# A quarter of the V rows of two tiles moves from TensorE to ScalarE and GpSimd, in a hybrid decoder step

## The reference

```python
q = (hb @ wq).astype(jnp.float32).reshape(chunk, PEER_HEADS, 2, PEER_HALF)
s = jnp.einsum('nhcd,hckd->nhck', q, sk)
sv, si = lax.top_k(s, PEER_TOPK)
...
expert = i1 * N_KEYS + i2
g = jax.nn.softmax(cs, axis=-1)
act = jax.nn.gelu(jnp.einsum('nd,nhkd->nhk', hb, u_tab[expert]).astype(jnp.float32), approximate=False)
return jnp.einsum('nhk,nhkd->nd', (g * act).astype(hb.dtype), v_tab[expert])
```

## Time and profile before

| | us |
|---|---|
| three runs, median | 3117.82 |
| lowest and highest | 3115.86, 3122.54 |
| the profiled execution | 3122.88 |
| its span, first to last instruction | 3121.1 |

### The profile page before, as it was taken

How to read it: one execution, slowest core, us unless ns; L and a number is a source line. 1 busy time by engine, 2 the same in 40 slices (tenths; PEclk the granted TensorE clock), 3 DMA queues, 4 the chain that set the end, 5 groups by cost and what they waited for, 6 DMA issues and landing times.

```text
span 3121.1 us, 28094 instructions
## 1 busy us (share of the span) xinstructions
PE 2647.9 (85%) x7627; PEld 1310.5 (42%) x7627; DVE 2101.5 (67%) x5113; ACT 1275.5 (41%) x3700; POOL 1172.5 (38%) x1088
## 2 busy tenths in 40 slices
PE   6688989999988887888798978887898977777777
PEld 5456546555544443333344434332344432222222
DVE  3444675678676766687766777777666766677666
ACT  1112343555444343444433344444444444444444
POOL 2000343333443333444343344444344444444442
PEclk9889999999999999999999999998999999999999
DMA  8845999999999999999999999999999999999998
GB/s 304 295 171 207 419 395 398 410 394 396 409 408 420 420 420 387 419 421 421 390 406 411 402 376 414 422 421 385 421 419 420 409 403 416 418 417 410 421 412 344
DMA packets 181215, 1221.28 MB, mean 391 GB/s; under 512 B 21340, under 2 KB 21608, under 8 KB 47033
## 3 DMA queue, kind: packets, MB, share of 16 engines
q0 software_dynamic: 150528, 1124.11, 87.8%
q1 hardware_dynamic: 30529, 95.38, 8.4%
HBM read 1213.68 MB, written 38.37 MB: 401 GB/s over the span
## 4 chain that ended last, share of the span: by engine, by line
DMA 41%; PE 32%; ACT 8%; DVE 7%; issue 3%; POOL 1%; DVEq 0%; ACTq 0%; POOLq 0%
DMA RING<-in_peer_uv,idx 41%; PE PSUM L1041 24%; PE PSUM L796 6%; DVE RING L1587 4%; ACT diag L1202 2%; ACT L1198 2%; ACT gate L1199 1%; ACT L1178 1%; ACT act_h L1198 1%; DVE H L1244 1%; POOL RING L747 1%; PE PSUM L1032 1%; PE PSUM L778 0%; PE PSUM L807 0%; DVE H L1257 0%
## 5 line engine op out<-in xcount | busy, mean ns | idle before, releaser
L1041 PE MATMUL PSUM<-RING,diag 128*128 128x512 f32 (+1 forms) x4160 | 1995.4, 620 | 400.3 <-ACT diag L1202 395.1
L1587 DVE CUSTOM_DVE_ANT_0 RING<-RING,H 128x1024 f32<-128x1024 f32 x1032 | 1264.1, 1225 | 777.1 <-DMA RING<-in_peer_uv,idx 770.5
L747 POOL DMA_INDIRECT RING<-in_peer_uv,idx x1024 | 1130.5, 1104 | 1672.2 <-PE PSUM L1041 1565.8
L1041 PEld LDWEIGHTS PSUM<-RING,diag 128*128 128x128 f32 (+1 forms) x4160 | 754.7, 192 | 1523.0 <-ACT diag L1202 843.7
L1198 ACT ACTIVATE act_h<-dots 128x1 f32<-128x1 f32 x1040 | 207.5, 199 | 1053.6 <-DVE dots L1587 1051.4
L1202 ACT ACTIVATE diag<-ident,gate 128x128 f32<-128x128 f32 x1024 | 411.1, 402 | 34.7 <-PE PSUM L1041 1.2
L796 PE MATMUL PSUM<-HT,WCH 128*128 128x264 f32 (+1 forms) x1664 | 390.6, 389 | 6.5 <-DMA WCH<-in_w_in_ab 5.0
L796 PEld LDWEIGHTS PSUM<-HT,WCH 128*128 128x128 f32 x1664 | 317.3, 193 | 80.4 <-issue 29.7
L1199 ACT ACTIVATE gate<-act_h,ex 128x1 f32<-128x1 f32 x1024 | 301.5, 294 | 33.3
L1086 ACT ACTIVATE YT<-PSUM 128x264 f32<-128x264 f32 (+2 forms) x68 | 27.1, 399 | 245.5 <-PE PSUM L796 234.2
L1198 ACT ACT_TABLE_LOAD x91 | 116.8, 1283 | 4.4 <-DVE dots L1587 2.8
(11 more groups left out here) (189 smaller groups left out, 1439.8 us busy)
## 6 DMA issues: line engine op xcount, KB each, us to landing
WCH<-in_peer_wq SPq DMA_DIRECT2D x64, 512.0 KB, 7.9
WCH<-in_w_in_ab SPq DMA_DIRECT2D x48, 512.0 KB, 7.7
RING<-in_peer_uv,idx POOLq DMA_INDIRECT x1024, 12.5
out_win_k_sample<-in_state_win_k POOLq DMA_DIRECT2D x8, 2046.0 KB, 10.4
out_win_v_sample<-in_state_win_v POOLq DMA_DIRECT2D x8, 2046.0 KB, 9.6
WCH<-in_w_out_ab SPq DMA_DIRECT2D x16, 512.0 KB, 6.9
RING<-in_state_win_k SPq DMA_DIRECT2D x16, 256.0 KB, 8.8
RING<-in_state_win_v SPq DMA_DIRECT2D x16, 256.0 KB, 4.2
```

The source lines that it names most:

```text
L747: pool.indirect_dma_start(rows[:, use % SLOTS, :], None, peer_uv.rearrange("l e n -> (l e) n"), bass.IndirectOffsetOnAxis(ap=at, axis=0),) ...
L1041: last = nc.tensor.matmul(PSUM[0:out_n, accumulator(n) + half, :], diag[:, use % DIAGS, 0:out_n], rows[:, use % SLOTS, D + half * 512:D + ...
L1587: V.tensor_tensor_reduce(out=u, in0=u, in1=row, scale=1.0, scalar=0.0, op0=ALU.mult, op1=ALU.add, accum_out=dots[:, tau % SETS, k:k + 1]). ...
```

## The change

In tiles 0 and 1 of layer 0, uses with `use % 4 == 1` no longer go to TensorE. That is 64 of the 256 uses. ScalarE scales their v half in its slot by the gate, instead of making a diagonal. GpSimd adds the scaled row to the residual `X` directly, just before it issues the gather that takes the same slot again, seven uses later. TensorE skips these uses; its diagonals and `v_freed` count the others only. Both adds to `X`, GpSimd's among themselves and VectorE's at the end of the tile, are ordered by the new semaphore `v_added`.

```diff
+SHARE = 4
...
+def by_pool(use):
+
+    return use < BT * PH * TOP and use % SHARE == 1
+
+
+def pool_rows(use):
+
+    return sum(by_pool(n) for n in range(use))
...
+            def add_row(use):
+
+                tau, k = divmod(use, TOP)
+                x = X[:, tau // PH + 1, :]
+                n = pool_rows(use)
+                pool.wait_ge(row_scaled, n + 1)
+                if n:
+                    pool.wait_ge(v_added, n)
+                nc.gpsimd.tensor_tensor(x, rows[:, use % SLOTS, D:ROW], x, ALU.add).then_inc(v_added, 1)
+
             def gather(tau, k):
 
                 use = first(tau) + k
-                if use >= SLOTS:
-                    pool.wait_ge(v_freed, use - SLOTS + 1)
+                old = use - SLOTS
+                if old >= 0 and by_pool(old):
+                    add_row(old)
+                    pool.wait_ge(v_added, pool_rows(old) + 1)
+                elif old >= 0:
+                    pool.wait_ge(v_freed, old - pool_rows(old) + 1)
...
             def accumulate(n, tau, k, out_n, opens, closes):
 
                 use = first(tau) + k
-                pe.wait_ge(diag_ready, use + 1)
+                if by_pool(use):
+                    return
+                row = use - pool_rows(use)
+                pe.wait_ge(diag_ready, row + 1)
                 for half in range(2):
-                    last = nc.tensor.matmul(PSUM[0:out_n, accumulator(n) + half, :], diag[:, use % DIAGS, 0:out_n],
+                    last = nc.tensor.matmul(PSUM[0:out_n, accumulator(n) + half, :], diag[:, row % DIAGS, 0:out_n],
...
-                if use >= DIAGS:
-                    act.wait_ge(v_freed, use - DIAGS + 1)
-                nc.scalar.activation(diag[:, use % DIAGS, 0:n], selector, ACT.Copy,
+                if by_pool(use):
+                    act.wait_ge(landed[use % SLOTS], 16 * (use // SLOTS + 1))
+                    v = rows[:, use % SLOTS, D:ROW]
+                    nc.scalar.activation(v, v, ACT.Copy, scale=gate[:, st, column]).then_inc(row_scaled, 1)
+                    return
+                row = use - pool_rows(use)
+                if row >= DIAGS:
+                    act.wait_ge(v_freed, row - DIAGS + 1)
+                nc.scalar.activation(diag[:, row % DIAGS, 0:n], selector, ACT.Copy,
                                      scale=gate[:, st, column]).then_inc(diag_ready, 1)
...
-                dve.wait_ge(v_freed, first(tau) + steps(tau))
+                done = first(tau) + steps(tau)
+                dve.wait_ge(v_freed, done - pool_rows(done))
+                if n < BT:
+                    dve.wait_ge(v_added, pool_rows(done))
```

More of the change, by code:

```diff
@@ L493, in build @@
         ring_cleared = sem("ring_cleared")
+        row_scaled = sem("row_scaled")
+        v_added = sem("v_added")
         prev_saved = sem("prev_saved")
```

## The result

| | before | after |
|---|---|---|
| median us (fastest to slowest) | 3118.02 (3115.86 to 3122.54) | 3155.11 (3148.68 to 3164.2) |
| profiled execution, its span | 3122.88, 3121.1 | 3151.84, 3150.1 |
| start of the add at the end of tile 0, of tile 1 | 687.2, 1048.3 | 700.4, 1077.8 |

The ratio is 1.0112, with a 95% interval of 1.0089 to 1.0135: 35 us slower. (The ratios in this document come from all runs of both kernels. They are not quotients of the medians, which differ by 37 us here.) The prediction was 3104 us, faster, in a range of 3090 to 3134, and the measured time lies above that range. All of the loss lies where the change is: the add of tile 0 starts 13 us later and that of tile 1 29.5 us later, and the difference of the two spans is 29.0 us.

The account below looks back on a forecast made before the run. Transfers or TensorE were taken to set the pace, with TensorE late with slots in tiles 0 and 1. Relief of -17 us and +3 us for VectorE's port gave -14, hence 3104 us against the median; range 3090 to 3134.

Parts of the forecast that it names:

- What bounds the kernel: Tiles 0 and 1 (299 to 1022 us): TensorE is late with the slots, so the transfer rate falls by some 4%.
- rival N: Tiles 0 and 1: the transfers have nothing to give, or gaps only move to VectorE; 3118 us, chance 0.22.
- What comes back as time: 300 to 900 us: the rate rises from 403 to 415 GB/s, 17 us less.
- TensorE's busy time: 299 to 1022 us: 64 rows removed take 119 us off 677.7, leaving 559 us.
- Scaling and add: 64 rows of tiles 0 and 1: 1.15 us per scaling on ScalarE, 2.5 us per add on GpSimd.
- the longer queue of GpSimd: Before every fourth gather: slots come back 1.4 us later by work alone, covered by about 4.6 us of queueing.
- VectorE's port: Tiles 0 and 1: GpSimd adds contend with VectorE's dot products; only 700 to 800 us pays, 3 us.
- The adds to the residual: Ends of tiles 0 and 1: VectorE's add also waits for GpSimd's last add, but nothing waits in effect.
- what lies behind: After 1048 us: led by the transfers, everything just moves forward, with later tiles' lengths unchanged.
- Rival S: Tiles 0 and 1: every fourth refill is delayed beyond the queueing that hides it; 3133 us, chance 0.23.
- its signs: Tiles 0 and 1: longer L1587 or idle time before it, landings below 9 us, GpSimd waiting for the scalings.

Follow-up runs that it names:

- memset: Changed kernel with GpSimd's add replaced by a memset of about the same length, which reads nothing: 3121.43 us, 1.0000 against before.
- plain work: The same 64 rows scaled and added by VectorE itself, two uses later, nothing extra on ScalarE or GpSimd: 3142.32 us, 1.0068 against before.
- dead adds: Kernel before, TensorE taking all rows, with a GpSimd add of dead data ahead of every fourth gather of the first two tiles: 3157.06 us, 1.0112.

## Why the prediction was wrong

**What bounds the kernel: wrong in the reading.** "So TensorE is late with the slots, the queue of transfers gets short, and the rate falls by some 4%." TensorE did hold the chain, at 44.5%, and the queue did get longer when it was relieved (the median gather landed in 11.6 us without the add, for 10.0), but the rate rose from 403 to 405 GB/s. The engines' share of 0.99, which I put under rival N, was the sign: outside the gaps the transfers were full with 3.5 in flight as with 4.

**What comes back as time: -17 us, measured -4 (-9 to +1)** by the kernel without the add, and nothing without scaling too. This term was mis-sized by a factor of four or more. It was taken from means over 600 us, where the slices of 15 us would have shown gaps, at least two of which another wait makes.

**TensorE's busy time: 559 us forecast, 596 without the add.** About 21 of these 37 us are the clock's; the sum had taken the cost of a record at the old clock.

**Scaling and add: right** as durations, 1.15 and 2.41 us (forecast 2.5), and the longer queue of GpSimd costs nothing, as said.

**VectorE's port: +3 us, measured +35** (add against memset, 1.0112 against 1.0000). This is the step that turned the sign. The mechanism was in the prediction, with about the right upper size of a lock (2.5 us; the longest product took 2.8 longer). Its amount was set too low: VectorE's busy time grew by 94 of the 160 us that a full exclusion would give, where I had said less than half. But above all the rule failed that I used for its price, that only the stretch in which VectorE's sum passes 100% pays. VectorE's idle time was mostly waiting for landings, at moments of its own, and could not cover the locks. TensorE waits for VectorE in the attention (37.0 us in L805, for 2.2 before and 18.6 with the memset) and gives back the slots later. 82 us on VectorE cost 20 us even as plain work.

**The adds to the residual, and what lies behind: right.** The tiles behind 1048 us kept their lengths within about 1 us.

**Rival S had the right side, at 3133 us, with half of its mechanism.** Its locks were real, but it priced the held refill of the fourth slot; a held refill without reads costs nothing (memset, 1.8 us). Of its signs only the longer L1587 came: from 300 to 900 us the median gather landed in 10.7 us, and GpSimd did not wait for the scalings. Rival N was right on the transfers and wrong for the whole.

The rule cited from the Trainium skill (SBUF — State Buffer, "Who interferes with whom") held in every run that bears on it: reads of GpSimd hold a VectorE instruction with two SBUF inputs for the whole instruction (up to 4.03 us for 1.225), or are held by it (up to 3.29 us for 2.36), and a write alone does not. That the one which starts first wins, as the Trainium skill has it, the recorded starts can neither show nor refute. I had named it and then discounted it by half. The estimate of 2.25 us for the add, from the Trainium skill (GPSIMD Engine Reference, section 3.1), is close to the 2.41 measured.

## What to carry to other kernels

An elementwise GpSimd instruction that reads SBUF beside a VectorE stream of two-input instructions can cost VectorE up to its own length (here 94 us for 154 us of adds). Price it as VectorE work, and then do not take VectorE's idle time for cover where its instructions stand in a round trip of slots. Before relief of an engine is credited with bandwidth, look at the rate in slices short enough to show gaps, and at the busy share of the DMA engines: an engine can hold most of the chain while the transfers it feeds are full.

## What the hardware showed beyond that

A GpSimd memset, which left the products alone, held small one-input instructions of VectorE. From the timeline of the memset's kernel, VectorE and then GpSimd:

```profile
375.72 1.41 DVE L1639 TENSOR_SCALAR ex<-ex,rsum 128x16 f32<-128x16 f32 x1
```

```profile
375.28 1.82 POOL L760 MEMSET RING<- 128x2048 f32 x1
```

The TENSOR_SCALAR of 16 columns takes 0.23 us elsewhere, and here ended with the memset, at 377.1. And two GpSimd adds of 512 columns back to back held a waiting product through both in 41 of 42 cases. The lock costs GpSimd as well: with dead adds in front of the gathers 25 of 64 adds were lengthened, the longest to 3.43 us for 2.36.
